# Expert gather of a PEER layer: VectorE's waits on its own increments, the choice of rows in 19 steps, the share moved

## The reference

```python
def block(xb):                                          # 256 tokens
    q = (xb @ w_q).reshape(TOK_BLOCK, PEER_HEADS, 2, PEER_DHALF)
    s = jnp.einsum('thcd,hcnd->thcn', q, sub_keys)      # 8 heads, 2 halves, 128 keys
    top_s, top_i = lax.top_k(s, K)                      # K = 16
    cand = top_s[:, :, 0, :, None] + top_s[:, :, 1, None, :]
    best_s, best_c = lax.top_k(cand.reshape(TOK_BLOCK, PEER_HEADS, K * K), K)
    i1 = jnp.take_along_axis(top_i[:, :, 0], best_c // K, axis=-1)
    i2 = jnp.take_along_axis(top_i[:, :, 1], best_c % K, axis=-1)
    e = (i1 * PEER_NKEYS + i2).reshape(TOK_BLOCK, PEER_HEADS * K)
    gate = jax.nn.softmax(best_s, axis=-1).reshape(TOK_BLOCK, PEER_HEADS * K)
    u = expert_u[e]                                     # 128 rows of 1024 floats a token
    act = jax.nn.gelu(jnp.einsum('td,ted->te', xb, u), approximate=False)
    coef = (gate * act.astype(jnp.float32)).astype(xb.dtype)
    return jnp.einsum('te,ted->td', coef, expert_v[e])
```

## Time and profile before

| what | value |
|---|---|
| median of 3 runs | 1630.85 us (1630.5 to 1631.46) |
| profiled execution | 1632.98 us, its span 1631.3 us |
| mean granted TensorE clock | 0.934 of full speed |
| busy over the span | PE 84%, DVE 65%, ACT 34%, POOL 33% |
| HBM read | 406.54 MB |
| software DMA queue (the gathers) | 269.52 MB, 42.8% of the 16 engines' span |

### The profile page before, as it was taken

One profiled execution on the slowest core, in us unless ns is written; L12 is line 12 of the kernel. 1 busy time (PEld: TensorE's weight loads), 2 busy tenths in 40 slices (PEclk: granted clock), 3 DMA queues, 4 the chain that ended last, 5 costly groups with the idle time before them and its releaser, 6 DMA issues.

```text
span 1631.3 us, 22696 instructions
## 1 busy us (share of the span) xinstructions
PE 1366.1 (84%) x8206; PEld 985.8 (60%) x8206; DVE 1064.8 (65%) x2068; ACT 560.9 (34%) x1048; POOL 533.3 (33%) x620
## 2 busy tenths in 40 slices
PE   8999999997999999999999567574858739667775
PEld 7989998896998888788888423221323213222231
DVE  5657765488775568877767967555575758655444
ACT  6656654466664454222441221110111111202111
POOL 8200010000000000000003656666676666667663
PEclk9999999998999999999999879797989969899887
DMA  8445665544565553311456999999999999999996
GB/s 248 148 140 166 188 201 185 177 149 136 171 203 181 195 167 104 104 54 56 153 170 238 383 348 369 355 355 407 352 373 356 356 343 375 370 395 373 355 361 268
DMA packets 184018, 408.96 MB, mean 251 GB/s; under 512 B 10674, under 2 KB 91868, under 8 KB 183916
## 3 DMA queue, kind: packets, MB, share of 16 engines
q0 software_dynamic: 74096, 269.52, 42.8%
q1 hardware_dynamic: 109516, 137.06, 26.0%
q10 hardware_dynamic: 304, 1.05, 0.2%
HBM read 406.54 MB, written 1.05 MB: 250 GB/s over the span
## 4 chain that ended last, share of the span: by engine, by line
PE 43%; issue 20%; DVE 19%; POOL 8%; another core or an unknown queue 7%; ACT 1%; DMA 1%; POOLq 0%; DVEq 0%; ACTq 0%
PE banks L2209 11%; PE banks L2210 11%; PE banks L2211 11%; DVE arena L2058 4%; POOL arena L916 4%; PE banks L2453 3%; POOL wring L916 2%; PE banks L2550 1%; PE banks L2444 1%; POOL h_raw L916 1%; DVE w_a_low L1415 1%; DVE h_raw L1663 1%; DVE arena L1990 1%; DVE arena L1986 1%
## 5 line engine op out<-in xcount | busy, mean ns | idle before, releaser
L916 POOL DMA_INDIRECT arena<-in_expert_u_dram,eidx x117 | 110.6, 945 | 692.3 <-DVEq L2038 637.0
L1415 DVE TENSOR_TENSOR w_a_low<-wring,w_a_high 128x1024 fp32r<-128x1024 f32 x192 | 235.2, 1228 | 122.1 <-ACT w_a_high L960 117.2
L2725 PE MATMUL banks<-arena 128*128 128x512 f32 x416 | 206.9, 642 | 92.9 <-issue 45.0
L960 ACT ACTIVATE w_a_high<-wring 128x1024 fp32r<-128x1024 f32 x192 | 201.1, 1052 | 124.3 <-PE banks L2211 123.6
L2209 PE MATMUL banks<-h_high,w_a_high 128*128 128x256 f32 (+1 forms) x832 | 238.1, 286 | 0.9 <-DVE h_low L1437 0.7
L2210 PE MATMUL banks<-h_low,w_a_high 128*128 128x256 f32 (+1 forms) x832 | 235.0, 282 | 0.0
L2211 PE MATMUL banks<-h_high,w_a_low 128*128 128x256 f32 (+1 forms) x832 | 233.5, 281 | 0.0
L1379 ACT ACTIVATE arena<-ident,arena 128x128 f32<-128x128 f32 x238 | 83.1, 394 | 437.0 <-remote 195.9
L2725 PEld LDWEIGHTS banks<-arena 128*128 128x128 f32 x416 | 81.1, 204 | 216.6 <-issue 173.8
L2725 PE MATMUL banks<-wring,arena 128*128 128x512 f32 x308 | 154.6, 646 | 54.0 <-issue 42.1
L2058 DVE CUSTOM_DVE_ANT_0 arena<-arena,banks 128x1024 f32<-128x1024 f32 x117 | 142.8, 1221 | 60.6 <-DMA arena<-in_expert_u_dram,eidx 20.1
(11 more groups left out here) (399 smaller groups left out, 2347.3 us busy)
## 6 DMA issues: line engine op xcount, KB each, us to landing
wring<-in_mlp_w_dram SPq DMA_DIRECT2D x64, 1024.0 KB, 5.3
wring<-in_w_in_dram SPq DMA_DIRECT2D x19, 1024.0 KB, 5.6
wring<-in_sb_w_qkv_dram SPq DMA_DIRECT2D x11, 1024.0 KB, 6.8
wring<-in_rg_w_in_dram SPq DMA_DIRECT2D x8, 1024.0 KB, 5.4
wring<-in_w_q_dram SPq DMA_DIRECT2D x8, 1024.0 KB, 5.3
wring<-in_sb_w_o_dram SPq DMA_DIRECT2D x4, 1024.0 KB, 5.4
wring<-in_rg_w_o_dram SPq DMA_DIRECT2D x4, 1024.0 KB, 5.1
wring<-in_w_o_dram SPq DMA_DIRECT2D x4, 1024.0 KB, 7.4
```

Source lines behind the costliest of these rows:

```text
L916: g.indirect_dma_start(out=grow(j), out_offset=None, in_=(expert_u, expert_v)[which][0], in_offset=bass.IndirectOffsetOnAxis(ap=eidx[:, tt ...
L960: a.activation(unit(n, 0), raw_unit(n), ACT.Copy).then_inc(w_high, 1)
L1415: v.tensor_tensor(unit(n, 1), raw_unit(n), unit(n, 0).bitcast(F32), ALU.subtract).then_inc(w_split, 1)
L2725: last = mm(y_banks[tt][half][:, :], diag[:, n % DIAGS, :], grow(j)[:, 512 * half:512 * (half + 1)], start=False, stop=True, skip_group_ch ...
```

## The change

1. `dot_row` no longer waits for its own increment. It writes its unused elementwise result to one of four scratch rows (two in block 0) and waits, before it, for the product that used the same scratch row, four (two) products back. The last product of a block still waits for itself before `dots_ready`. At the start of block 1 there is a wait until the scores of tile 1 are copied out, as their inputs' space is scratch from then on.
2. `choose` is cut into 19 steps. In blocks 1 to 6 step s runs after the product r = 2 + s; in block 0, four steps run after each of the products 9 to 13; the first choice, ahead of block 0, runs its steps one behind the other. Each step begins with `settle()`, and only the last instruction of a group that depends on nothing in the group is marked. That is 18 marks a block in place of 48, beside `gsel_ready` and `eidx_ready`. The arithmetic is the same.
3. `share` becomes `shares`, three steps after the products r = 24, 25 and 26 of the block's own pass, and `coefficients`, one instruction at r = 1 of the next pass. ScalarE's order is unchanged.
4. GpSimd's increments of `slot_seen` are gone, its waits are not.

```diff
-        junk = area(20552, D)
+        junk_first = [area(20552, D), yacc[0]]
+        junk = [area(20552, D), area(4096, D), area(5120, D), area(27942, D)]
...
                 if before:
                     pool.wait_ge(slot_free[j], before)
-                    pool.sem_inc(slot_seen, 1)
...
-            def choose(b, part, heads=(0, 1)):
+            def choose(b, step, heads=(0, 1)):
...
+                settle()
+                if step == 0:
                     wait_out(dve, f"sc{tt}_{h0}")
-                    first8(topv[:, hc], topi[:, hc], (sc, scores1)[tt][:, hc], rest)
+                    for k in range(2 * nh):
+                        last = v.max(vals[:, k, 0:8], scored[:, k, :])
+                    mark(last)
+                elif step == 1:
+                    for k in range(2 * nh):
+                        v.max_index(idx[:, k, 0:8], vals[:, k, 0:8], scored[:, k, :])
+                        last = v.match_replace(rest[:, k, :], vals[:, k, 0:8], scored[:, k, :], NEG)
+                    mark(last)
...
+                elif step == 5:
+                    for i in range(nh):
+                        v.max_index(at[:, i, 0:8], best[:, i, 0:8], sums[:, i, :])
+                        last = v.match_replace(rest2[:, i, :], best[:, i, 0:8], sums[:, i, :], NEG)
+                    mark(last)
...
+                elif step == 17:
+                    mark(v.tensor_copy(eidx[:, tt, TOPK * h0:TOPK * h0 + n], picked(i1f)))
                 else:
-                    index_of(h0, nh, colf, 1, i2f)
...
                     dve.sem_inc(eidx_ready, 1)
...
+            CHOICE = 19
...
             def dot_row(b, r):
...
                 j, before = gather_row(b, 0, r)
+                scratch = junk if b else junk_first
+                back = len(scratch)
+                if n == BSEL:
+                    wait_out(dve, *[f"sc1_{2 * m}" for m in range(4)])
+                if r >= back:
+                    jb, before_b = gather_row(b, 0, r - back)
+                    dve.wait_ge(slot_free[jb], before_b + 1)
                 dve.wait_ge(row_loaded[j], 16 * (before + 1))
-                ins = v.tensor_tensor_reduce(out=junk, in0=grow(j), in1=f_bank[tt][:, :], scale=1.0, scalar=0.0,
-                                             op0=ALU.mult, op1=ALU.add, accum_out=dots[:, tt, c:c + 1])
-                ins.then_inc(slot_free[j], 1)
-                dve.wait_ge(slot_free[j], before + 1)
-
-            def share(b):
+                v.tensor_tensor_reduce(out=scratch[r % back], in0=grow(j), in1=f_bank[tt][:, :], scale=1.0, scalar=0.0,
+                                       op0=ALU.mult, op1=ALU.add,
+                                       accum_out=dots[:, tt, c:c + 1]).then_inc(slot_free[j], 1)
+                if r == BSEL - 1:
+                    dve.wait_ge(slot_free[j], before + 1)
+                    dve.sem_inc(dots_ready, 1)
+
+            def shares(b, step):
...
+                settle()
+                if step == 0:
+                    dve.wait_ge(gsel_exp, b + 1)
+                    mark(v.tensor_reduce(psm[:, 0:2], g3, AX.X, ALU.add))
+                elif step == 1:
+                    mark(v.reciprocal(psm[:, 0:2], psm[:, 0:2]))
+                else:
+                    mark(v.tensor_tensor(g3, g3, psm[:, 0:2].unsqueeze(2).broadcast_to([P, 2, TOPK]), ALU.mult))
+
+            def coefficients(b):
...
+                settle()
                 dve.wait_ge(gelu_ready, b + 1)
-                link(v.tensor_tensor(coef[:, tt, c0:c0 + BSEL], coef[:, tt, c0:c0 + BSEL],
-                                     gsel[:, tt, c0:c0 + BSEL], ALU.mult))
-                dve.sem_inc(coef_ready, 1)
+                v.tensor_tensor(coef[:, tt, c0:c0 + BSEL], coef[:, tt, c0:c0 + BSEL],
+                                gsel[:, tt, c0:c0 + BSEL], ALU.mult).then_inc(coef_ready, 1)
...
-                    picks = (2, 7, 12, 17, 22) if b else (9, 10, 11, 12, 13)
-                    if b < BLOCKS - 1 and r in picks:
-                        choose(b + 1, picks.index(r))
+                    if 0 < b < BLOCKS - 1 and 2 <= r < 2 + CHOICE:
+                        choose(b + 1, r - 2)
+                    if b == 0 and 9 <= r < 14:
+                        for step in range(4 * (r - 9), min(4 * (r - 8), CHOICE)):
+                            choose(1, step)
+                    if b < BLOCKS and 24 <= r < 27:
+                        shares(b, r - 24)
...
                     if b > 0 and r == LAG - 1:
-                        share(b - 1)
+                        coefficients(b - 1)
```

More of the change, by code:

```diff
@@ L1981, in natural @@
                 link(v.tensor_tensor(f_bank[tt][:, :], xres[:, tt, :], gffn_row, ALU.mult))
-            def first8(vals, idx, src, rest):
-                for r_ in range(src.shape[1]):
-                    mark(v.max(vals[:, r_, 0:8], src[:, r_, :]))
-                settle()
-                for r_ in range(src.shape[1]):
-                    mark(v.max_index(idx[:, r_, 0:8], vals[:, r_, 0:8], src[:, r_, :]))
-                    mark(v.match_replace(rest[:, r_, :], vals[:, r_, 0:8], src[:, r_, :], NEG))
-                settle()
@@ L1993, in second8 @@
-            def second8(vals, idx, rest):
-                for r_ in range(rest.shape[1]):
-                    mark(v.max(vals[:, r_, 8:16], rest[:, r_, :]))
-                settle()
-                for r_ in range(rest.shape[1]):
-                    mark(v.max_index(idx[:, r_, 8:16], vals[:, r_, 8:16], rest[:, r_, :]))
-                settle()
-            def choose(b, part, heads=(0, 1)):
+            def choose(b, step, heads=(0, 1)):
                 tt, h0, nh = b // 4, 2 * (b % 4) + heads[0], len(heads)
@@ new lines, in times @@
+                def times(half):
+                    for i in range(nh):
+                        oo = o_[:, TOPK * i:TOPK * (i + 1), :]
+                        last = v.tensor_tensor(oo, oo, topf[:, 2 * (h0 + i) + half, :].unsqueeze(1).broadcast_to(
+                            [P, TOPK, TOPK]), ALU.mult)
+                    mark(last)
+                settle()
+                if step == 0:
+                    wait_out(dve, f"sc{tt}_{h0}")
+                    for k in range(2 * nh):
[6 more added lines that the diff above has]
+                    mark(last)
+                elif step == 2:
+                    for k in range(2 * nh):
+                        last = v.max(vals[:, k, 8:16], rest[:, k, :])
+                    mark(last)
+                elif step == 3:
+                    for k in range(2 * nh):
+                        v.max_index(idx[:, k, 8:16], vals[:, k, 8:16], rest[:, k, :])
+                    for i in range(nh):
+                        last = v.tensor_tensor(sums[:, i, :].rearrange("p (i j) -> p i j", j=TOPK),
+                                               vals[:, 2 * i, :].unsqueeze(2).broadcast_to([P, TOPK, TOPK]),
+                                               vals[:, 2 * i + 1, :].unsqueeze(1).broadcast_to([P, TOPK, TOPK]),
+                                               ALU.add)
+                    mark(last)
+                elif step == 4:
+                    v.tensor_copy(topf[:, hc], idx)
+                    for i in range(nh):
+                        last = v.max(best[:, i, 0:8], sums[:, i, :])
+                    mark(last)
+                elif step == 5:
+                    for i in range(nh):
+                        v.max_index(at[:, i, 0:8], best[:, i, 0:8], sums[:, i, :])
+                        last = v.match_replace(rest2[:, i, :], best[:, i, 0:8], sums[:, i, :], NEG)
+                    mark(last)
+                elif step == 6:
+                    for i in range(nh):
+                        last = v.max(best[:, i, 8:16], rest2[:, i, :])
+                    mark(last)
+                elif step == 7:
+                    for i in range(nh):
+                        v.max_index(at[:, i, 8:16], best[:, i, 8:16], rest2[:, i, :])
@@ L2120, in _ @@
             for h in range(2):
-                for part in range(5):
-                    choose(0, part, (h,))
+                for step in range(CHOICE):
+                    choose(0, step, (h,))
             for b in range(BLOCKS + 1):
```

82 lines of the change are left out of this document (35 added, 47 removed).

## The result

| | before | after |
|---|---|---|
| median of 4 runs | 1630.67 us (1630.45 to 1631.46) | 1619.99 us (1618.75 to 1621.06) |
| profiled execution, its span | 1632.98, 1631.3 us | 1618.75, 1617.0 us |
| ratio, 95% interval | | 0.9933 [0.9916, 0.9951] |

The change is 10.7 us faster; the forecast was 7 us, 1624. The profiled pair is 14.3 us apart in the span: that execution of the new kernel is its fastest, and that of the kernel before, 1632.98, is slower than its four runs.

What follows compares the result with a forecast made beforehand. Bound: GpSimd's gather issue, stopped when its 25-slot ring waits for late readers. Stops 5 us plus block 0 2 us took 7 us off 1632.98, giving 1626.0; from the median 1630.85, 1623.9, forecast as 1624. Range 1604 to 1637.

Steps and rivals of the forecast that it cites:

- What bounds the kernel: Gather from 968 us: GpSimd issues each 1.245 us, but stands still 86 us in 14 stops, held by its 25-slot ring.
- VectorE's passage through the choice: Choice in 19 steps: the 20.3 us passage shrinks to 13 or so; four GpSimd stops, 24 us if all went.
- What TensorE takes back: TensorE's late increments still stop GpSimd; runs grow to 40 us, sparing 0.85 stops at 6 us: 5.1 us.
- Products without their own wait: 256 dot products wait for the product four (block 0: two) back: 0 alone, at most 3 us a block.
- The share's own part: Block boundary, coefficients: three of four instructions go to r = 24 to 26; counted as nothing, between 0 and 8 us.
- A mark costs 0.69 us: Choice on VectorE: an increment costs up to 0.69 us, so three fewer take 2.1 us off the 8.71 wait.
- GpSimd's increments cost nothing: Gather issue: 512 or so increments go, but the pace of 1.245 us stays: 0.
- The first rival: All engines' increments share one path, so with fewer all stops come later: 37 us less, 1594; chance 0.13.
- Block 0: Share at r = 24 parks VectorE 13.4 us before product 25: 2 us gained, between 5 lost and 5 gained.
- the start: First choice, 864 to 873.6 us, has quick waits: 0, within 0.5 us.
- the third rival: Slower through parked VectorE after block 0's product 24: new 5 us stop, old 8.5 us one untouched, 1636; chance 0.16.
- the second rival: Gather stops move but stay as many, now all behind TensorE: within 3.3 us; chance 0.19.

Runs made afterwards that it cites:

- chip 6: Number of the chip of one of three slower sets, in which the kernel before took 1636.7 to 1637.7 us.
- the four kernels built on after: The changed kernel with marks back (0.9936), two tiny copies per choice step (0.9938), the first tile's end later (0.9940), or 16 diagonals (0.9934).
- the quick set: Changed kernel run again, unchanged, in a set whose kernel before took some 1554 us: ratio 1.0008; with GpSimd's slot_seen increments put back 1.0009.
- the products' run: Kernel before with only the products' waits for their own increment replaced by a wait on the product four back: 1.0000 twice, both in quick sets.

## Why the prediction was right, and where not

- **What bounds the kernel: right.** Nearly all of the gain behind block 0, 9.9 of 11.0 us, is in GpSimd's stops.
- **VectorE's passage through the choice: right that it made the stops, not shown that the 19 steps alone removed them.** Four stops on VectorE's products were to go; the four came to 23.3 us (I had said 24), each at the product behind part 2, and 2.2 us are left. With the choice alone none stands at that place. But with only GpSimd's increments out none stands there either.
- **What TensorE takes back: the step that was mis-sized.** I let the runs grow to 40 us as without a choice, so that 0.85 stops of 6 us were spared: 5.1 us of 24 stay. Measured: 21.1 us removed, 11.3 taken back, 9.9 stay. I had predicted 12 or 13 long stops; there are more of them, 20 against 15 when those within 8 us are one, but 3.8 us over the usual interval and not 5.7, with 28 us of issuing to each and not 37 (I had assumed 6 and 40). That a stop's length is a constant was the wrong assumption. The executions of chip 6 give the same picture, 76 to 77 us in each of the four kernels built on after.
- **Products without their own wait: zero, untested where it matters.** Both runs fell in sets without late increments. The share's own part was not measured at all.
- **A mark costs 0.69 us: wrong.** In late stretches VectorE's instructions stand 0.70 us apart, marked or not. The sum used it for 2.1 us off one wait; 30 marks a block put back moved nothing that could be seen. What the 19 steps bring, as far as the traces show, is that a wait is not stood through.
- **GpSimd's increments cost nothing: wrong**, 0.9950 alone, 5 to 11 us: the term that I put at 0 is as large as the whole forecast of 7. I had reasoned from its pace of 1.245 us, which indeed didn't change (1.246 on average between stops in the changed kernel, 1.249 before). The gain must be in the stops, and why is open: that profile has 79.6 us of them against 85.0, but from another set, of whose kernel before there is no profile. The first rival (all increments share one path) gains weight from it. The marks speak against it only weakly: at GpSimd's price, 8 us for 65 increments a block, 30 marks would cost 3.8 us, hardly more than the runs can tell. A rule that holds for both would be that an engine's own instructions are what delays its own reports; GpSimd's 520 increments are instructions of their own, and the marks are not. That was not tested.
- **Block 0: right in direction, part of it chance.** 2 us gained were forecast at this place. 3.3 came, but 1.7 of them already at the first gather: 0.8 by an earlier chance of ScalarE, 0.3 by a shorter first choice, and 0.6 by the increment that GpSimd no longer makes ahead of the first gather (1.13 or 1.14 us from the last cast's start to it in every profile with the increment that was looked at, 0.51 or 0.52 in every one without). I had put the start within 0.5. In four kernels of one set with this same start the first gather began anywhere from 872.3 to 876.1, so only the 0.6 is clear of chance. The park was 9.2 us. Where it was longer and the stop at 946 was there, the third rival's place was right and its price wrong: the old stops behind it shrank from 8.5 us to 1.3 to 1.7, and from the first gather to the 63rd it took 92.8 to 93.9 us, where it took 94.6 before and 91.7 in the result's profile.
- **Slower, or no change: not here.** But in the quick set the second rival's number is the result, 1.0008, by a mechanism that I did not have: there are no stops to move.
- **The sum was near by luck in part.** 7 us were forecast and 10.7 came, by terms that don't stand as priced: the choice's 5 us fit its own run (3 to 9), TensorE's answer was sized wrong, and GpSimd's increments were missing. How the 10.7 us divide between the parts is not shown.

The Trainium skill's "the semaphore costs nothing extra" ("VectorE: DVE Perf Modes", section "The DRAIN you can't avoid") holds better than I gave it credit for: the run with all marks back agrees with it, even though instructions stand 0.70 us apart in late stretches. GpSimd's increments, which are instructions of their own, are another matter (0.9950).

## What to carry to other kernels

When a ring stops its issuer, book every stop on the reader of the slot that it waited for, before and after; the sum by reader says at once which engine's lateness is left, and a part of what one reader gives up the next one takes back. Put independent work between an increment and its wait before counting increments. Then ask of each stop when the reader had really finished: 0.8 us before, and the reader is late; 20 to 29 us before, and its increment is, which making the reader faster does not cure. Measure in more than one set before you tune against a lateness: this one is some 85 us of stops in one and absent in another.

## What the hardware showed unexpectedly

- The same program took 1630.7, 1637 and 1554 us in different sets. The stops are what differs: 102 us of them over the whole gather before, 8 in the first quick profile of the products' run. 15 of the 94 us come back at the end, as the quick run takes 30.8 us from the last gather's start to the program's end and the slower one 15.9. Both move 414 to 422 GB/s while gathers flow (419 and 422 in the 8 us windows at 1109 and 1117 in the trace of after), so a full transfer queue alone does not make increments late. What differs between the sets stays open; it need not be the chip.
- In a late stretch VectorE's instructions are slowed to one each 0.70 us or twice that, marked or not, and GpSimd goes on up to 29 us after the end of the TensorE row that it waits for. The Trainium skill ("NOTIFIC — the notification-queue block", section "Overflow: three behaviours, one of which stalls the engine") describes one way in which an engine's own reports can hold it up. No run here shows whether it is that.
- A gather issued by GpSimd under a VectorE sum of two SBUF inputs took 1.5 to 2.0 us in 17 cases (1.83 in the one shown), and 0.94 as a rule otherwise; sums into PSUM did not do it.
